# An fp32 hybrid encoder layer: four raw weight slots, operands one a unit, later low parts

## The chip, the cores and the metric

The kernel runs on one core of a Trainium2 chip. The metric is the device time of one execution in microseconds (us); lower is better. Five engines run side by side and meet at semaphores: TensorE (PE) multiplies, VectorE (DVE), ScalarE (ACT) and GpSimd (POOL) work on elements, SyncE (SP) issues transfers.

## The reference

One layer over 2048 prompt frames with 16 meta tokens ahead of them and 32 frames of a running stream, 1024 channels, fp32:

```python
proj = rmsnorm(x) @ w_in                      # x_a, x_b, g_a, g_b, 1024 columns each
y_a  = rg_lru(conv4(x_a))                     # two 128-wide gates a head, then a scan over time
y_b  = pool_mix(x_b)                          # window means 2, 4, 8, 16, then a grouped product
x    = x + (sig(g_A) * (y_a @ w_br_a) + sig(g_B) * (y_b @ w_br_b)) @ w_out
g, u = split(rmsnorm(x) @ w_gu)               # 2816 columns each
x    = x + (silu(g) * u) @ w_down
y    = rmsnorm(x) * final_g
```

Outputs are y and the convolution, scan and pooling states of both streams.

## The kernel before

**Split products.** Every operand is cut into a high part (rounded to fp32r) and a low part (the rest), and a product takes three matmuls a 128-deep step: high by high, high by low, low by high. Weights arrive raw from memory by SP into `wraw`, three slots of 1024 columns; ACT makes the high part (L878, `split_hi`), DVE the low part (L1720, `split_lo`) in `wring`, three places of 1024 columns (a fourth, `wextra`, in the mixer), or in `wlast`, four places of 768 columns over the same memory. PE waits for the low part. SP sends for raw slot n when the low part of slot n-3 is made. ACT may write a place of the ring when PE has used it up; these waits stand in the program at `ahead` and `ahead_of`, right where the product that frees the place ends.

**Mixer.** Five blocks of 416 or 432 columns, each with the stages xa (convolution input), gates, ga, gb, a, xb, b and o, eight products of 24 matmuls each. In stage o (output projection) of a block but the last, ACT per product m waits for DVE's addition of the product to `main` (L1857), squares the sum for the next norm (`square`, L909), makes the next block's high operand (`normed`, L931), and splits a weight. DVE per product splits a weight, makes the next operand and the low part of the one before (`normalize`, L1360, L1364), adds (L1857), and adds up the square (`square_sum`, L1342).

**Feed-forward.** Three tiles of two halves of 348 or 346 columns; the products of 2 by 2 blocks take 7 block products, not 8 (`PROD`). `gate_up(s, p)` is one of 11 pairs of hidden tiles: 7 products (units) of 24 matmuls, k = 0 to 6. ACT and DVE drain them (`tap_out` L1106, `add_out` L1625), take the SiLU (L1147) and make the seven hidden operands with high and low parts in `hcomb` (DVE L1672 to L1698; the fourth and fifth low parts are L1696 and L1698). `down(s, g)` follows pair 2g+2 and uses pairs 2g and 2g+1, in 14 units of 12 matmuls; the last, g = 4, uses three pairs with the 768-wide weights, 14 units of 18. It starts before pair 10 is ready: for its first three units PE makes the sums over two pairs, then it waits for pair 10's parts and adds the third. `add_down` (L1711) adds each unit to `xacc`. PSUM is four pairs of banks in turn, so a unit needs the addition of the unit four before it.

**Beside it.** While pair 10 and the last down group run, the next tile's seven operands `ycomb` are made from `ys` in memory: POOL loads quarters of `ys` into `work` (L609), DVE makes four differences (`operand_diff`: T1 L1578, T3 L1580, T2 L1583, T4 L1586), ACT the high parts (`operand_hi`, L1095), DVE the low parts (`operand_lo`, L1569). The tables `BESIDE_B`, `BESIDE_O`, `BESIDE_GU` and `BESIDE_DN` say at which unit. The last quarter is sent for when the sixth low part is made. In the first two pairs of a tile the norm of the tile before is finished: squares, a column sum on PE, a root, one reciprocal of 692 columns (`norm_invert`, L1612), and eight scalings (`finish`, L1617) at the units in `FINISH`.

The lines in `down(s, 4)` that set how much PE does ahead of the wait for pair 10:

```python
                    for k, mp in steps[:3]:
                        hold(("dn", s, g, mp, k, 0))
                        part(k, mp, (0, 1))
                pe.wait_ge(h_hi, 4 * n)
                pe.wait_ge(h_lo, 4 * n)
```

## Time and profile before

| what | value |
| --- | --- |
| time, median of 3 runs | 2750.82 us (2748.52 to 2753.92) |
| the profiled execution: time, span | 2748.8 us, 2747.0 us |
| PE matmuls | 15404, busy 2681.8 us (98% of the span) |
| DVE, ACT, POOL busy | 2059.0 (75%), 1358.9 (49%), 192.9 us (7%) |
| granted TensorE clock, mean | 0.995 |
| transfers | 486.10 MB, mean 177 GB/s |
| chain that ended last | PE 76%, DVE 12%, issue 5%, ACT 4%, DMA 2% |

The span runs from the first to the last instruction. A row of the timeline gives start, duration, engine, line, operation, tiles written and read, and in square brackets the idle time of that engine ahead of it with what ended it. "issue" is time that the profile puts down to no one.

### The profile page before, as it was taken

What the parts mean: (1) busy time and instruction counts of PE and PEld (TensorE: products, weight loads), DVE (VectorE), ACT (ScalarE), POOL (GpSimd) and SP (SyncE); (2) the same over time, 40 slices, a digit from 0 to 9 for tenths busy, and PEclk for the clock granted to TensorE, in tenths of its full rate; (3) what the DMA queues carried; (4) which work ended last, traced back from release to release, by engine and by line L of the source; (5) the groups of instructions that cost most, each with busy time, mean ns of one, the idle gap of its engine ahead of it and who ended that gap; (6) DMA issues with size and microseconds to landing.
All of it is one profiled execution on the core that took longest, in us unless ns stands there. A gap on an engine that the chain in (4) does not pass through costs nothing.

```text
span 2747.0 us, 39191 instructions
## 1 busy us (share of the span) xinstructions
PE 2681.8 (98%) x15404; PEld 2651.8 (97%) x15404; DVE 2059.0 (75%) x2723; ACT 1358.9 (49%) x1822; POOL 192.9 (7%) x369
## 2 busy tenths in 40 slices
PE   8999999999999999999999999999999999999995
PEld 7999999999999999999999999999999999999995
DVE  7868787788878877887777676688667688676666
ACT  6743484358436743663454344454434345344442
POOL 2000101020101011101100000001000000000000
PEclk9999999999999999999999999999999999999998
DMA  7453567546765767566564444456444454644443
GB/s 241 132 186 115 192 222 268 190 162 228 253 202 172 235 220 233 172 231 210 199 205 133 144 138 138 141 160 235 130 144 136 139 160 163 207 137 139 131 131 99
DMA packets 149254, 486.10 MB, mean 177 GB/s; under 512 B 16464, under 2 KB 34000, under 8 KB 149072
## 3 DMA queue, kind: packets, MB, share of 16 engines
q1 hardware_dynamic: 106224, 345.21, 38.5%
q0 software_dynamic: 32336, 121.92, 12.9%
q10 hardware_dynamic: 10512, 16.46, 2.0%
q8 instruction: 124, 2.03, 0.3%
q14 instruction: 58, 0.48, 0.1%
HBM read 419.01 MB, written 64.51 MB: 176 GB/s over the span
## 4 chain that ended last, share of the span: by engine, by line
PE 76%; DVE 12%; issue 5%; ACT 4%; DMA 2%; SPq 0%; DVEq 0%; ACTq 0%
PE ps L704 75%; DVE wring L1720 2%; ACT wring L878 1%; DVE work L1672 1%; DMA work<-ys 1%; ACT work L1147 1%; DVE work L1625 1%; DVE ga L1841 1%; DVE xacc L1711 1%; DVE work L1674 1%; DVE tmp L1839 1%; DMA wraw<-dwm 1%; DMA wraw<-draw 1%; DVE hcomb L1678 1%; DVE nrstd L1612 0%
## 5 line engine op out<-in xcount | busy, mean ns | idle before, releaser
L704 PE MATMUL ps<-ycomb,wring 128*128 128x346 f32 (+1 forms) x5544 | 884.7, 321 | 9.6 <-DVE wring L1720 5.7
L704 PEld LDWEIGHTS ps<-ycomb,wring 128*128 128x128 f32 x5544 | 880.8, 188 | 11.6 <-DVE wring L1720 6.9
L1720 DVE TENSOR_TENSOR wring<-wraw,wring 128x1024 fp32r<-128x1024 f32 x529 | 644.9, 1220 | 261.8 <-ACT wring L878 260.1
L878 ACT ACTIVATE wring<-wraw 128x1024 fp32r<-128x1024 f32 x529 | 557.1, 1054 | 443.9 <-PE ps L704 422.6
L704 PE MATMUL ps<-xhi,wring 128*128 128x416 f32 (+1 forms) x1728 | 478.3, 353 | 11.8 <-DVE wring L1720 8.9
L704 PE MATMUL ps<-yhi,wring 128*128 128x416 f32 x1568 | 429.5, 351 | 0.4 <-DVE ylo L1364 0.4
L704 PEld LDWEIGHTS ps<-xhi,wring 128*128 128x128 f32 x1728 | 326.4, 189 | 16.6 <-issue 12.4
L704 PE MATMUL ps<-hcomb,wring 128*128 128x346 f32 (+1 forms) x2016 | 325.6, 322 | 4.7 <-DVE xacc L1711 4.7
L704 PEld LDWEIGHTS ps<-hcomb,wring 128*128 128x128 f32 x2016 | 320.6, 188 | 8.0 <-DVE xacc L1711 8.0
L704 PE MATMUL ps<-xlo,wring 128*128 128x416 f32 (+1 forms) x864 | 305.2, 353 | 0.0
L704 PEld LDWEIGHTS ps<-yhi,wring 128*128 128x128 f32 x1568 | 294.3, 188 | 2.8 <-issue 0.7
L704 PE MATMUL ps<-ylo,wring 128*128 128x416 f32 x784 | 275.1, 351 | 0.0
L1711 DVE TENSOR_TENSOR xacc<-ps,xacc 128x692 f32<-128x692 f32 (+1 forms) x210 | 179.0, 872 | 39.0 <-PE ps L704 39.0
L1106 ACT ACTIVATE work<-ps 128x692 f32<-128x692 f32 (+1 forms) x99 | 74.1, 748 | 193.9 <-PE ps L704 193.7
L704 PEld LDWEIGHTS ps<-xlo,wring 128*128 128x128 f32 x864 | 163.1, 189 | 2.8
L704 PE MATMUL ps<-xhi,wextra 128*128 128x416 f32 (+1 forms) x576 | 162.1, 352 | 0.0
L704 PEld LDWEIGHTS ps<-ylo,wring 128*128 128x128 f32 x784 | 147.1, 188 | 1.7
L1625 DVE TENSOR_TENSOR work<-ps,work 128x692 f32<-128x692 f32 (+1 forms) x99 | 86.8, 877 | 71.0 <-PE ps L704 71.0
L704 PE MATMUL ps<-yhi,wextra 128*128 128x416 f32 x480 | 134.7, 352 | 0.0
L704 PE MATMUL ps<-hcomb,wlast 128*128 128x346 f32 (+1 forms) x756 | 122.7, 322 | 7.8 <-DVE wlast L1720 5.0
L704 PEld LDWEIGHTS ps<-hcomb,wlast 128*128 128x128 f32 x756 | 119.9, 188 | 10.4 <-issue 10.4
L704 PEld LDWEIGHTS ps<-xhi,wextra 128*128 128x128 f32 x576 | 108.2, 188 | 1.4
(236 smaller groups left out, 2922.8 us busy)
## 6 DMA issues: line engine op xcount, KB each, us to landing
wraw<-dwm SPq DMA_DIRECT2D x247, 512.0 KB, 3.9
wraw<-sgu SPq DMA_DIRECT2D x132, 512.0 KB, 3.3
wraw<-graw SPq DMA_DIRECT2D x99, 512.0 KB, 3.5
wraw<-sdn SPq DMA_DIRECT2D x48, 512.0 KB, 3.6
pbuf<-graw POOLq DMA_DIRECT2D x22, 1024.0 KB, 7.5
sgu<-pbuf POOLq DMA_DIRECT2D x22, 1024.0 KB, 6.1
wraw<-fused SPq DMA_DIRECT2D x40, 512.0 KB, 3.3
wraw<-draw SPq DMA_DIRECT2D x36, 512.0 KB, 3.7
```

Of the source, the lines that this page charges most:

```text
L704: mm = nc.tensor.matmul(out, wt[:, c * P:(c + 1) * P], x, start=(first and q == 0), stop=(last and q == 2), skip_group_check=chain)
L878: A(ring(n)[:, 0, 0:c], wraw[:, n % RAW, 0:c], ACT.Copy, scale=cst[:, PSC, name[2]:name[2] + 1] if name[0] == "w" else 1.0).then_inc(w_hi, 1)
L1106: A(work[:, first:first + 8:7, 0:TH[s]], both(name, TH[s]), ACT.Copy).then_inc(cleared[BANK[name] // 2], 1)
L1147: A(work[:, 0:3, 0:w], work[:, 0:3, 0:w], ACT.Silu).then_inc(silu3, 1)
L1625: V.tensor_tensor(c, both(name, TH[s]), c, ADD).then_inc(cleared[BANK[name] // 2], 1)
L1672: V.tensor_tensor(work[:, 7:10, 0:w], work[:, 7:10, 0:w], work[:, 0:3, 0:w], MUL).then_inc(h_mult, 1)
L1674: V.tensor_tensor(work[:, 3:5, 0:w], work[:, 8:10, 0:w], work[:, 7:9, 0:w], SUB).then_inc(h_diff, 1)
L1678: V.tensor_tensor(hl[:, 0:2, :], work[:, 7:10:2, 0:w], hh[:, 0:2, :].bitcast(f32), SUB).then_inc(h_lo, 1)
L1711: V.tensor_tensor(out, both(name, w), out, ADD).then_inc(cleared[BANK[name] // 2], 1)
L1720: V.tensor_tensor(ring(n)[:, 1, 0:c], wraw[:, n % RAW, 0:c], ring(n)[:, 0, 0:c].bitcast(f32), SUB).then_inc(w_lo, 1)
L1839: V.tensor_tensor(tmp[:, 3 + 4 * (m % 2), 0:LW], bank(name)[:, 0:LW], gb[:, m, 0:LW], MUL).then_inc(drained[BANK[name]], 1)
L1841: V.tensor_tensor(ga[:, m, :], ga[:, m, :], tmp[:, 3 + 4 * (m % 2), 0:LW], ADD).then_inc(merged, 1)
```

## The change

1. `wraw` gets a second view, `rawlast`, of four slots of 768 columns in the same 12 units of memory. A planner (`places`) gives each slot its place and the slot whose low part must be made before it is loaded. For the last down group that is four slots back, not three; with four raw semaphores by n % 4.
2. In `down(s, 4)` PE takes four units with two pairs ahead of the wait for pair 10, not three.
3. `hidden_rest` holds the last two low parts of a pair. Where a down group of two pairs follows the pair, DVE runs it behind that group's first two additions.
4. The operand tables: operand 0 a unit earlier, one entry a unit in the last down group and in stage o, and T4 moved to the next tile's first unit, operand 6 to its third. In pairs' units DVE takes operands behind `add_out`; in the last down group and the last block's stage o ACT takes them behind the weight split.
5. In stage o of blocks 0 to 3 ACT squares behind the next operand and the split, and DVE adds the square up one product later.
6. The reciprocal is taken in two halves of 346 or 348, at units (1, 0) and (1, 1) of a tile, and in a row at the end of the program; `FINISH` starts one unit later for its first four entries. The last block's last quarter is sent for behind store 6, not 5.

The core of the diff; its two parts on `ahead` are ACT's, in stage o and in the last down group:

```diff
-FINISH = {(1, 1): (0,), (1, 2): (1,), (1, 3): (2,), (1, 4): (3,), (2, 0): (4, 5), (2, 1): (6, 7)}
+FINISH = {(1, 2): (0,), (1, 3): (1,), (1, 4): (2,), (1, 5): (3,), (2, 0): (4, 5), (2, 1): (6, 7)}
-BESIDE_O = {2: ("T1", "T3"), 3: ("T2", 4), 4: (2,), 5: (3,), 7: ("T4",)}
-BESIDE_GU = {2: (0,), 4: (5,)}
-BESIDE_DN = {1: (1,), 4: ("T1", "T3"), 5: ("T2", 4), 7: (2,), 8: (3,), 11: ("T4",)}
+BESIDE_O = {2: ("T1", "T3"), 3: ("T2",), 4: (4,), 5: (2,), 6: (3,)}
+BESIDE_GU = {1: (0,), 4: (5,)}
+BESIDE_DN = {1: (1,), 3: ("T1",), 4: ("T3",), 5: ("T2",), 6: (4,), 7: (2,), 8: (3,)}
...
-PLACE, PREV = ring_places()
+PLACE, PREV = places(16, RING, True)
 RELEASE = list(itertools.accumulate(PREV, max))
+RAW_PLACE, RAW_PREV = places(12, RAW, False)
+RAW_RELEASE = list(itertools.accumulate(RAW_PREV, max))
...
-                if n >= RAW:
-                    sp.wait_ge(w_lo, n - RAW + 1)
+                if RAW_RELEASE[n] >= 0:
+                    sp.wait_ge(w_lo, RAW_RELEASE[n] + 1)
...
-                    for k, mp in steps[:3]:
+                    for k, mp in steps[:4]:
...
-                    if width == 3 and i < 3:
+                    if width == 3 and i < 4:
...
+                    if b < NB - 1 and m < KT - 1:
+                        normed(b + 1, m + 1)
+                    ahead(b, "o", m)
                     if b < NB - 1:
                         act.wait_ge(*drain(("o", b, m)))
                         square("n2", b, m, main[:, m, :])
-                        if m < KT - 1:
-                            normed(b + 1, m + 1)
                     else:
                         operands(0, BESIDE_O, m)
-                    ahead(b, "o", m)
...
+                        ahead_of("dn", s, i, j)
                         if s < NT - 1 and i == LASTG:
                             operands(s + 1, BESIDE_DN, j)
-                        ahead_of("dn", s, i, j)
...
-            def norm_invert(s):
-                w = 2 * TH[s]
+            def norm_invert(s, half):
+                w = TH[s]
                 dve.wait_ge(*clear(("n3", s, 0)))
-                V.reciprocal(nrstd[:, 0:w], nrstd[:, 0:w]).then_inc(n_rstd, 1)
+                V.reciprocal(nrstd[:, half * w:half * w + w], nrstd[:, half * w:half * w + w]).then_inc(n_rstd, 1)
...
                 if (p, k) == (0, 0):
+                    operand_diff(s, "T4")
+                elif (p, k) == (0, 2):
                     operand_lo(s, 6)
...
+                if early or not before_dn(s, p):
+                    hidden_rest(s, p)
...
                             add_down(s, i, j, 0)
                             add_down(s, i, j, 1)
+                            if j == 0:
+                                hidden_rest(s, 2 * i + 2)
```

Three places of DVE's order, in tile 0. First, the end of pair 10 (`ycomb` operand low parts, `work<-ps` the additions of `add_out`, `wlast` the last down group's weights), before:

```order
L1569 TENSOR_TENSOR ycomb<-work,ycomb 128x4x346
L1720 TENSOR_TENSOR wring<-wraw,wring 128x1024 x2
L1569 TENSOR_TENSOR ycomb<-work,ycomb 128x4x346
L1625 TENSOR_TENSOR work<-ps,work 128x2x348 x2
L1672 TENSOR_TENSOR work<-work 128x1044
```

and now:

```order
L1580 TENSOR_TENSOR ycomb<-work,ycomb 128x4x346
L1743 TENSOR_TENSOR wring<-wraw,wring 128x1024 x3
L1636 TENSOR_TENSOR work<-ps,work 128x2x348
L1580 TENSOR_TENSOR ycomb<-work,ycomb 128x4x346
L1636 TENSOR_TENSOR work<-ps,work 128x2x348
L1685 TENSOR_TENSOR work<-work 128x1044
```

The second operand low part stood ahead of both additions and stands between them. Second, pair 2's end and the first down group, before:

```order
L1720 TENSOR_TENSOR wring<-wraw,wring 128x1024
L1696 TENSOR_TENSOR hcomb<-work,hcomb 128x348
L1698 TENSOR_TENSOR hcomb<-work,hcomb 128x348
L1711 TENSOR_TENSOR xacc<-ps,xacc 128x2x348 x2
L1720 TENSOR_TENSOR wring<-wraw,wring 128x1024
```

and now:

```order
L1743 TENSOR_TENSOR wring<-wraw,wring 128x1024
L1734 TENSOR_TENSOR xacc<-ps,xacc 128x2x348 x2
L1719 TENSOR_TENSOR hcomb<-work,hcomb 128x348
L1721 TENSOR_TENSOR hcomb<-work,hcomb 128x348
L1743 TENSOR_TENSOR wring<-wraw,wring 128x1024
```

The two low parts went behind the two additions. Third, the end of the last down group and the start of tile 1 (`work<-work 128x4x346` is T4), before:

```order
L1711 TENSOR_TENSOR xacc<-ps,xacc 128x2x348 x2
L1586 TENSOR_TENSOR work<-work 128x4x346
L1720 TENSOR_TENSOR wring<-wraw,wring 128x1024
L1711 TENSOR_TENSOR xacc<-ps,xacc 128x2x348
L1720 TENSOR_TENSOR wring<-wraw,wring 128x1024
L1711 TENSOR_TENSOR xacc<-ps,xacc 128x2x348
```

and now:

```order
L1734 TENSOR_TENSOR xacc<-ps,xacc 128x2x348 x2
L1743 TENSOR_TENSOR wring<-wraw,wring 128x1024
L1734 TENSOR_TENSOR xacc<-ps,xacc 128x2x348
L1743 TENSOR_TENSOR wring<-wraw,wring 128x1024
L1734 TENSOR_TENSOR xacc<-ps,xacc 128x2x348
L1743 TENSOR_TENSOR wring<-wraw,wring 128x1024
L1597 TENSOR_TENSOR work<-work 128x4x346
```

T4 went behind all the group's additions and three splits of the next tile's weights.

## Rows read from the trace of the kernel before

**Rows 1.** Who PE waited for, whole span: us in total, times, longest us.
```profile
PE ps L704 <- DVE wring L1720: 14.6, 5, 8.9
PE ps L742 <- issue: 11.0, 1, 11.0
PE ps L704 <- DVE xacc L1711: 4.7, 12, 1.3
PE ps L704 <- DVE xlo L1364: 3.0, 2, 2.5
PE ps L704 <- DVE ylo L1364: 0.4, 1, 0.4
```

**Rows 2.** Chain that ended last: a stretch of ten mixer products.
```profile
462.50 45.36 PE ps L704 x240
```

**Rows 3.** DVE's timeline, stage o of block 3.
```profile
1097.31 0.58 DVE L1857 TENSOR_TENSOR main<-ps,main 128x416 f32<-128x416 f32 x1
...
1102.21 0.58 DVE L1857 TENSOR_TENSOR main<-ps,main 128x416 f32<-128x416 f32 x1
...
1104.89 1.23 DVE L1720 TENSOR_TENSOR wring<-wraw,wring 128x1024 fp32r<-128x1024 f32 x1 [0.89 <-ACT wring L878]
```

**Rows 4.** ACT's timeline, the same product.
```profile
1102.82 0.55 ACT L909 ACTIVATE sq<-main 128x416 f32<-128x416 f32 x1 [2.85 <-DVE main L1857]
...
1103.81 1.04 ACT L878 ACTIVATE wring<-wraw 128x1024 fp32r<-128x1024 f32 x1
```

**Rows 5.** DVE's timeline, end of pair 2 in tile 0.
```profile
1455.08 0.51 DVE L1696 TENSOR_TENSOR hcomb<-work,hcomb 128x348 fp32r<-128x348 f32 x1
...
1455.94 1.67 DVE L1711 TENSOR_TENSOR xacc<-ps,xacc 128x696 f32<-128x696 f32 x2
```

**Rows 6.** PE's timeline, first down group of tile 0.
```profile
1456.87 19.42 PE L704 MATMUL ps<-hcomb,wring 128*128 128x348 f32 x120 [0.32 <-DVE xacc L1711]
```

**Rows 7.** PE's timeline, pair 10 of tile 0 to tile 1's first pair.
```profile
1769.86 4.07 PE L704 MATMUL ps<-ycomb,wring 128*128 128x348 f32 x24 [1.35 <-DVE work L1625]
1775.45 5.99 PE L704 MATMUL ps<-hcomb,wlast 128*128 128x348 f32 x36 [1.52 <-DVE wlast L1720]
1782.74 20.28 PE L704 MATMUL ps<-hcomb,wlast 128*128 128x348 f32 x126 [1.30 <-issue]
1804.02 14.61 PE L704 MATMUL ps<-hcomb,wlast 128*128 128x348 f32 x90 [1.01 <-DVE wlast L1720]
1820.52 23.11 PE L704 MATMUL ps<-ycomb,wring 128*128 128x346 f32 x144 [1.88 <-DVE wring L1720]
```

**Rows 8.** DVE's timeline, the same stretch.
```profile
1767.32 1.60 DVE L1569 TENSOR_TENSOR ycomb<-work,ycomb 128x1384 fp32r<-128x1384 f32 x1 [3.46 <-ACT ycomb L1095]
1768.84 1.67 DVE L1625 TENSOR_TENSOR work<-ps,work 128x696 f32<-128x696 f32 x2
...
1807.76 0.95 DVE L1720 TENSOR_TENSOR wlast<-wraw,wlast 128x768 fp32r<-128x768 f32 x1
...
1810.92 0.95 DVE L1720 TENSOR_TENSOR wlast<-wraw,wlast 128x768 fp32r<-128x768 f32 x1
...
1817.73 1.60 DVE L1586 TENSOR_TENSOR work<-work 128x1384 f32<-128x1384 f32 x1 [2.62 <-DMA work<-ys]
```

**Rows 9.** ACT's timeline, the same stretch.
```profile
1778.68 0.84 ACT L878 ACTIVATE wlast<-wraw 128x768 fp32r<-128x768 f32 x1 [3.82 <-DMA wraw<-draw]
...
1800.01 1.36 ACT L1095 ACTIVATE ycomb<-work 128x1384 fp32r<-128x1384 f32 x1 [6.85 <-DVE work L1583]
```

**Rows 10.** POOL's timeline, the last quarter of `ys` for tile 1.
```profile
1811.30 0.75 POOL L609 DMA_DIRECT2D work<-ys  x1 [26.87 <-DVE ycomb L1569]
```

**Rows 11.** Groups by line and shape, PE in tiles 1 and 2: busy, mean ns, idle before.
```profile
L704 PE MATMUL ps<-ycomb,wring 128*128 128x346 f32 x3696 | 589.1, 321 | 7.3 <-DVE wring L1720 5.7 <-DVE work L1625 1.6
...
L704 PE MATMUL ps<-hcomb,wlast 128*128 128x346 f32 x504 | 81.8, 322 | 4.0 <-DVE wlast L1720 2.5 <-issue 1.4
```

**Rows 12.** DVE's timeline, the reciprocal in tile 1.
```profile
1854.94 4.50 DVE L1612 RECIPROCAL nrstd<-nrstd 128x696 f32<-128x696 f32 x1 [0.42 <-ACT nrstd L1122]
```

More of the change, by code:

```diff
@@ L205, in slot_width, with places @@
     return 768 if name[0] == "dn" and dn_units(name[2]) == 14 else KT * P
-LANDED = [16 * (n // RAW + 1) for n in range(NS)]
+LANDED = [16 * (n // 4 + 1) for n in range(NS)]
 NARROW = SLOT[("b", NB - 1, 0)]
-def ring_places():
-    last, places, before = [-1] * 16, [], []
+def places(units, wide, spare):
+    last, where, before = [-1] * units, [], []
     for n in range(NS):
         each = 3 if slot_width(n) == 768 else 4
-        spans = [range(each * q, each * q + each) for q in range(4 if each == 3 or n < NARROW else 3)]
+        spans = [range(each * q, each * q + each) for q in range(4 if each == 3 else wide + (spare and n < NARROW))]
         held = [max(last[u] for u in span) for span in spans]
         q = held.index(min(held))
-        places.append(q)
+        where.append(q)
         before.append(held[q])
@@ L224, in ring_places @@
             last[u] = n
-    return places, before
-PLACE, PREV = ring_places()
+    return where, before
+PLACE, PREV = places(16, RING, True)
 RELEASE = list(itertools.accumulate(PREV, max))
+RAW_PLACE, RAW_PREV = places(12, RAW, False)
+RAW_RELEASE = list(itertools.accumulate(RAW_PREV, max))
 def splits_after(k):
@@ L877, in split_hi @@
                 name, c = SLOTS[n], slot_width(n)
-                A(ring(n)[:, 0, 0:c], wraw[:, n % RAW, 0:c], ACT.Copy,
+                A(ring(n)[:, 0, 0:c], raw_of(n)[:, 0:c], ACT.Copy,
                   scale=cst[:, PSC, name[2]:name[2] + 1] if name[0] == "w" else 1.0).then_inc(w_hi, 1)
@@ L1661, in gate_up @@
                     beside(s, p, k)
-                    if p == PAIRS - 1 and s < NT - 1:
-                        operands(s + 1, BESIDE_GU, k)
                     if k == 1:
@@ L1676, in gate_up @@
                         V.tensor_tensor(work[:, 5, 0:w], work[:, 9, 0:w], work[:, 3, 0:w], SUB).then_inc(h_diff, 1)
+                    if p == PAIRS - 1 and s < NT - 1:
+                        operands(s + 1, BESIDE_GU, k)
                 dve.wait_ge(h_hi, 4 * n + 1)
@@ L1879, in _ @@
             norm_rest(NT - 1)
-            norm_invert(NT - 1)
+            for half in range(2):
+                norm_invert(NT - 1, half)
             for i in range(KT):
```

47 lines of the change are left out of this document (30 added, 17 removed).

## The prediction

> **What bounds the kernel now.** I read first how busy each engine is: PE computes during 98% of the span, and the change takes no matmul away and adds none. So all it can give is a part of PE's idle time, and the view of who PE waited for is the one to read. Of its long entries two lie outside the change: 8.9 us for the first weights of the program, and the 11.0 us before the last column sum, in which squares are added up on DVE [rows 1]. What is left are short waits, and each has its place in a timeline. There the reader looks at three things: which instruction ended PE's wait, what stood ahead of it on its own in-order engine, and what that one waited for. PE's pace between waits is needed as well: 240 matmuls of the mixer take 45.36 us, so a product of 24 takes 4.54 us [rows 2]; in the feed-forward 24 take about 3.86 us and 126 take 20.28 us, 0.161 us each, so a unit of 18 takes 2.90 us [rows 7].
>
> **Stage o of blocks 0 to 3.** DVE's additions to main follow each other at 4.90 us (1097.31 to 1102.21) [rows 3], PE's products at 4.54 us [rows 2]. The cause is a ring of waits over two engines: DVE adds, ACT squares the sum and only then makes the next operand and splits the weight (1102.82, split at 1103.81) [rows 4], DVE waits for that split (1104.89) [rows 3], then makes a low part and adds the next product. Each product falls back 0.36 us, eight make 2.9 us, and PE pays where the next block needs the last low part: 3.0 us in two waits and 0.4 us in a third [rows 1]. With the change ACT's split stands ahead of the square, so it starts when PE frees the place, about 0.6 us of addition and 0.5 us of square earlier, and the addition is no longer in the ring. From PE's end of a product, DVE is through with split, operand, low part and addition after about 1.0 + 1.2 + 1.1 + 0.6 = 3.9 us, under 4.54. I take all **3.4 us**; the bounds are 0 and 3.4. The added-up square is a product later, and its column sum is due only in the next block's gates, two stages on, which hides it.
>
> **Down groups of two pairs.** Twelve waits, 4.7 us in all, one of 1.3 and eleven of 0.24 to 0.38 [rows 1, 6]. PE's fifth unit needs the first addition; it starts at 1455.94 because the two low parts stand before it from 1455.08, 0.86 us [rows 5]. Moved behind, they free the bank 0.86 us sooner, and the small waits end. DVE's next split comes at the same time as before, since the same work precedes it. Who needs the two low parts? PE in the next down group, some 27 us on, and ACT's next use of that buffer a pair on. The long wait (1.3) keeps at least 0.4. I take **4.2 us**; bounds 3.3 and 4.7.
>
> **Tile 0, pair 10 and last down group.** Four waits: 1.35, 1.52, 1.30 and 1.01 us, 5.18 together [rows 7].
> - 1.35: unit 6 needs the addition of unit 4, which started at 1768.84, behind an operand's low part (1767.32) that had waited 3.46 us through ACT for its quarter [rows 8]. PE stopped at 1768.5 (1769.86 less 1.35), so unit 4 had ended a unit earlier, near 1764.7. Now the addition stands first, and the quarter is sent for a unit (3.86 us) sooner. This wait goes.
> - 1.52: this is the chain from unit 5's addition over SiLU, product and differences to the weight split. It is the second of the two at 1768.84 [rows 8] and so began near 1769.6, while unit 5 had ended at 1768.5. Freed of the first, it and the chain start 1.1 us sooner, and unit 6 ends 1.35 us sooner. PE starts the group at 1774.35, not 1775.45, after a wait of 1.95 us: the wait of 1.35 is gone, the one behind it grows, and 1.1 us is won.
> - 1.30: PE had three units of 12 ahead (5.99 us) and then waited for pair 10's last low part. That part was late because DVE's fourth weight split stood before it, and ACT's half of that split had waited 3.82 us for the raw weights [rows 9], which SP may send for only once the first wlast low part is made. With the fourth slot they are sent for one low part earlier and lie there in time. PE got the last part at 1782.74; with the chain 1.1 us sooner it is there by 1781.6 even if nothing of the transfer's wait is saved, and four units of 12 (twice 3.86 us) keep PE until 1774.35 + 7.7 = 1782.1. This wait goes.
> - 1.01: two differences in a row and operand 4 right behind the third; ACT stood 6.85 us for T2 with a weight split queued behind it [rows 9]. Now the split stands first and there is one operand a unit. What is late next is DVE: a split, an addition and an operand follow each other at 3.16 us (1807.76 to 1810.92) [rows 8] against PE's 2.90, from unit 3 to unit 8. Counting from the group's start, the split for unit 12 is ready near 35.1 us and PE wants it at 34.8. I put 0.4 us here; bounds 0 and 1.5.
>
> So 5.18 becomes 2.35: **2.8 us**.
>
> **Tiles 1 and 2, the same place.** Waits of 1.6 (addition), 2.5 (wlast) and 1.4 us (pair 10's parts), 5.5 together [rows 11]. In tile 1 the first weights of the group are split early, so both additions one operand sooner let the whole chain start over 2 us sooner; what stays is about 0.45 for the third unit's weights and 0.4 of DVE's lag. Tile 2 has no operands and keeps one 0.5, and loses the wait for pair 10. 5.5 becomes 1.35: **4.1 us**; bounds 2.5 and 4.8.
>
> **First pairs of tiles 1 and 2.** Four waits for weights, 5.7 us [rows 11]. Two (the longest 1.88 [rows 7]) stand behind T4, for which DVE waited 2.62 us on the quarter sent for at 1811.30 and landed at 1817.7 [rows 8, 10]. T4 now stands behind three splits. PE needs it, through ACT's tap_out, before unit 2 of the tile, 7.7 us in; that leaves over 5 us. Two stand behind the reciprocal of 4.50 us [rows 12]; a split between two halves of 2.25 us comes that much sooner, and the second half still ends before the next split is due. I take all **5.7 us**; bounds 3.5 and 5.7. FINISH a unit later puts a scaling ahead of an addition in unit 5, whose result is due only units later. In tile 0 the last quarter leaves over 4 us later than before, because operand 3 went from product 5 of stage o to 6 and behind ACT's split. From the end of product 6: split 1.0 [rows 4], operand high 1.4 [rows 9] and low 1.6, quarter 6.4 [rows 8, 10], T4 1.6 and tap_out some 0.8 (half of the two additions of 1.67) make 12.8 us. PE wants it after product 7, units 0 and 1 and whatever it waits at the tile's start: 4.5 + 7.7 = 12.2 us and that wait, which is DVE's last addition of stage o, some 0.7 us. That just fits: 0, at most 1 us lost.
>
> **The program's end.** Two halves of the reciprocal for one. Two instructions of 348 columns start 0.43 us apart [rows 5], one of 696 takes 0.83: the second instruction costs 0.03 us by these starts, 0.2 by whole durations (twice 0.51 less 0.83), and I take **0.1 us lost**. The Trainium skill (VectorE: DVE Perf Modes, on the TRN2 errata) speaks against such cuts: an instruction from SBUF pays a fixed cost each time, some 150 cycles, which at the engine's 0.96 GHz would be 0.16 us lost; the rows stand nearer to the lower value, and the sum would move by less than 0.1.
>
> **The sum.** 3.4 + 4.2 + 2.8 + 4.1 + 5.7 - 0.1 = 20.1 us. Against the profiled execution's own 2748.8 us that gives 2728.7. The median of the runs shown stands 2.0 us above it, and the same gain from there gives 2730.7. I forecast **2729.6 us**, between the two. A measurement of this kernel can tell about 0.2% (5.5 us) from no change.
>
> **Rivals.**
> - *DVE becomes the bound in the last groups.* DVE is busy for most of that stretch, and one operand a unit at 3.16 against 2.90 us leaves no air. If raw weights and semaphores add 0.3 us a unit over six units, some 2 us of waits in each of tiles 0 and 1 come back, with 1 to 2 us more where the first pairs are as full. For it: the lag is real. Against it: four ring places, three units of slack. 2729.6 + 6 = about 2735.5. Chance 0.22.
> - *The change doesn't do what it says.* The stage-o ring stays at 4.90 us since ACT's in-order queue still holds the square ahead of the next operand (3.4 us not won), and the two reciprocal halves leave the split late (2 us), and the down groups wait for the next addition (2 us). About 2737. Chance 0.07.
> - *Slower: T4 blocks DVE at the start of each tile.* T4 now sits in the pair in which DVE has the norm's sums too, and DVE is in order: while it waits for the quarter, splits and additions wait. Sums, splits and additions behind it have about 1 us of slack by unit 4. The quarter took 6.4 us alone [rows 10]. If it took 15 us because four raw loads and it were under way together, each of three tiles would lose 5 to 9 us: 20 gained, up to 27 lost, about 2756. It decides from a landing of some 13 us on. The Trainium skill (DMA: Bandwidth & Descriptors, on issuing engines) says that transfers from SP, ACT and POOL run on the same 16 engines and interleave, so a deeper raw queue could lengthen the quarter; 6.4 us here, with raw loads beside it, speaks against more than a few us. Chance 0.03.
> - Forecast, within 5 us: 0.66; the rest (0.02) is a small gain of under 5 us from several misses.
>
> **Range.** The low end takes all upper bounds (about 2 us more won) from the profiled execution: 2726. The high end takes the lower bounds and the first two rivals: 2739. Faster 0.94, same 0.03, slower 0.03.
>
> **What the changed profile would show.** DVE's additions in stage o 4.5 us apart and no wait for L1375's low part; no waits of 0.3 us for L1734 in down groups; 48 matmuls, not 36, at the head of the last group with no "issue" wait behind them, and a wait near 2 us ahead of it in tile 0 only; no wait at a tile's start; DVE's idle before T4 small in tiles 1 and 2 and some 3 us in tile 0; PE busy unchanged near 2682. I am wrong if new waits of over 1 us stand in units 8 to 13 of the last group, or in units 3 to 6 of a tile's first pair.

## The result, and the profile after

The changed kernel takes **2726.18 us** (median of 5 runs, 2723.72 to 2727.25); the kernel before, run beside it, 2749.32 us (5 runs, 2748.52 to 2753.92). The ratio is 0.991, with a 95% interval of 0.9897 to 0.9924. A second set of five runs gave 2726.32 us and 0.9917 (0.9903 to 0.993). So the change is faster by some 23 us. I had forecast 2729.6 with a low end of 2726: the direction was right, and the waits ended for the reasons given, but the price that the sum puts on a wait was too low. The central value is 3.4 us too high, and the measured time lies at the very low end of the range.

The profiled execution took 2727.25 us, with a span of 2725.5; that is 21.5 us less than the profiled execution of before (span 2747.0). The page's first part:

```profile
PE 2678.8 (98%) x15404; PEld 2652.8 (97%) x15404; DVE 2056.2 (75%) x2726; ACT 1360.2 (50%) x1822; POOL 191.2 (7%) x369
```

PE's busy time was 2681.8 us before. So of the 21.5 us, 18.5 left PE's idle time (2747.0 - 2681.8 = 65.2 before, 2725.5 - 2678.8 = 46.7 now) and 3.0 left its *busy* time, although the matmuls are the same 15,404. That second number is what the forecast has no term for: it had PE's busy time unchanged near 2682.

Who PE waited for, whole span (us in total, times, longest; answers to [rows 1]):

```profile
PE ps L753 <- issue: 11.0, 1, 11.0
PE ps L715 <- DVE wring L1743: 9.6, 2, 8.9
PE ps L715 <- DVE wlast L1743: 3.1, 3, 2.1
PE ps L715 <- ACT tmp L1031: 2.6, 1, 2.6
PE ps L715 <- DVE main L1880: 1.4, 1, 1.4
...
PE ps L715 <- DVE xacc L1734: 0.6, 1, 0.6
```

The waits for an operand's low part in stage o are gone, those for the down group's first addition went from 4.7 us in twelve to 0.6 in one, those for split weights (wring) from 14.6 in five to 9.6 in two, of which 8.9 is the program's first weights. The line with main is new in size (0.89 us before): the start of tile 0.

DVE's timeline in stage o of block 3 (answers to [rows 3]): the additions are 4.54 us apart, PE's own pace.

```profile
1095.23 0.59 DVE L1880 TENSOR_TENSOR main<-ps,main 128x416 f32<-128x416 f32 x1 [1.09 <-PE ps L715]
...
1099.77 0.59 DVE L1880 TENSOR_TENSOR main<-ps,main 128x416 f32<-128x416 f32 x1 [1.59 <-PE ps L715]
```

What released DVE is now PE, not ACT's split. DVE at the end of pair 2 (answers to [rows 5]); the addition stands ahead of the two low parts, and PE runs through:

```profile
1453.72 1.66 DVE L1734 TENSOR_TENSOR xacc<-ps,xacc 128x696 f32<-128x696 f32 x2
1455.30 0.51 DVE L1719 TENSOR_TENSOR hcomb<-work,hcomb 128x348 fp32r<-128x348 f32 x1
```

PE's timeline from tile 0's start to the last group of tile 2 (answers to [rows 7]; start, length, count, and in brackets the idle time before):

```profile
1365.11 23.15 PE L715 MATMUL ps<-ycomb,wring 128*128 128x348 f32 x144 [1.44 <-DVE main L1880]
1389.12 15.51 PE L715 MATMUL ps<-ycomb,wring 128*128 128x348 f32 x96 [0.21 <-DVE work L1636]
1405.28 6.95 PE L715 MATMUL ps<-ycomb,wring 128*128 128x348 f32 x42 [0.65 <-DVE wring L1743]
...
1770.74 41.30 PE L715 MATMUL ps<-hcomb,wlast 128*128 128x348 f32 x252 [2.05 <-DVE wlast L1743]
1811.87 23.00 PE L715 MATMUL ps<-ycomb,wring 128*128 128x346 f32 x144
...
2218.31 37.38 PE L715 MATMUL ps<-hcomb,wlast 128*128 128x346 f32 x228 [0.50 <-DVE wlast L1743]
...
2661.09 36.39 PE L715 MATMUL ps<-hcomb,wlast 128*128 128x346 f32 x228 [0.50 <-DVE wlast L1743]
```

There is one wait of 2.05 us ahead of tile 0's last group, then all 252 matmuls stand in one row, and tile 1 begins without a wait. The three last rows hold something smaller: the same 228 matmuls take 37.38 us in tile 1, where DVE makes the next tile's operands beside them, and 36.39 in tile 2, where it makes none. In tile 1, PE starts a matmul 0.39 us behind the one before, and the next 0.24 us behind that, at 2229.11, 2246.59 and 2249.75 us. The usual distance is 0.16, so each of the three places costs 0.31 us. Each stands just behind the end of a weight split on DVE, and DVE needs 3.17 us a unit there:

```profile
2245.49 0.95 DVE L1743 TENSOR_TENSOR wlast<-rawlast,wlast 128x768 fp32r<-128x768 f32 x1
...
2248.66 0.95 DVE L1743 TENSOR_TENSOR wlast<-rawlast,wlast 128x768 fp32r<-128x768 f32 x1
```

So PE does wait for DVE there, in gaps of 0.08 us that the timeline draws as no idle time. And DVE's timeline at tile 1's reciprocal (answers to [rows 12]):

```profile
1847.13 2.33 DVE L1623 RECIPROCAL nrstd<-nrstd 128x348 f32<-128x348 f32 x1 [0.21 <-ACT nrstd L1133]
1849.38 1.16 DVE L1743 TENSOR_TENSOR wring<-wraw,wring 128x1024 fp32r<-128x1024 f32 x1
1850.46 2.31 DVE L1623 RECIPROCAL nrstd<-nrstd 128x348 f32<-128x348 f32 x1
```

To see where the 21.5 us come from, I paired each matmul of one trace with the same matmul of the other and took the difference of their starts; where that difference steps, time was won or lost. Against the terms of the forecast:

| place | forecast, us | steps of the starts, us |
|---|---|---|
| stage o of blocks 0 to 3 | 3.4 | 0.66 + 0.68 + 2.80 = 4.1 |
| down groups of two pairs | 4.2 | ten of 0.51 to 0.60, one of 1.21, one of -0.19: 6.7 |
| tile 0, pair 10 and last group | 2.8 | 3.0 |
| tiles 1 and 2, the same place | 4.1 | 3.3 + 0.9 = 4.2 |
| first pairs of tiles 1 and 2 | 5.7 | 3.1 + 3.3 = 6.4 |
| tile 0's start and first pair | 0 | -0.53 - 0.69 - 0.90 = -2.1 |
| elsewhere | -0.1 | -0.7 (-0.8 of it in the first 100 us) |
| sum | 20.1 | 21.6 |

The terms of the last groups are net: what DVE's lag gives back there is taken off. The first 100 us are no term of the change. They hold 1.8 us less in a second profile of the same kernel (the next experiment).

### The profile page after: what moved, and what is told of

Its sections match the earlier page's. It is cut to its first block, busy times and chain, and to the rows that moved or that the text cites. A ratio compares the mean times of both kernels' runs of the same rounds, so it can differ in the third digit from the quotient of the medians.

```text
span 2725.5 us, 39194 instructions
## 1 busy us (share of the span) xinstructions
PE 2678.8 (98%) x15404; PEld 2652.8 (97%) x15404; DVE 2056.2 (75%) x2726; ACT 1360.2 (50%) x1822; POOL 191.2 (7%) x369
## 4 chain that ended last, share of the span: by engine, by line
PE 91%; DVE 4%; DMA 2%; issue 1%; ACT 1%; SPq 0%; DVEq 0%; ACTq 0%
PE ps L715 91%; DVE wring L1743 1%; DMA wraw<-draw 1%; DVE xacc L1628 0%; ACT wring L889 0%; DMA wraw<-graw 0%; DVE work L1685 0%; DVE work L1636 0%; ACT work L1158 0%; DVE work L1687 0%; DVE ntot L1613 0%; DVE hcomb L1693 0%; DMA wraw<-dwm 0%; DMA work<-ys 0%; DVE hcomb L1706 0%
```

## The experiments

There are two theories of why more was won than the idle rows hold. **Theory H**: ending a wait gives back its idle row *and* a fixed quarter of a microsecond around it. The rival: the idle rows are the whole price, and the rest is chance, or belongs to some other edit. Two more questions came from the table: whether tile 0's first pair really loses 2 us, and which edits carry which term.

**The same kernel again** (no edit).

> The changed kernel once more, unedited, timed against the kernel before. Theory A (the gain is the profiled 21.5 us, and the 23.1 us of the medians is how runs fall): gain between 20.5 and 24 us again, the profile's waits at the same places, PE's waits in the first pair of tile 0 (0.21 and 0.65 us idle) there again. Theory B (those waits are a chance of this one execution's transfers): they are gone, and the span is about 1.5 us shorter.

Measured: 2726.32 us (5 runs, 2725.36 to 2728.14), span 2723.6. PE's waits show no entry inside tile 0's first pair, so the waits of 0.21 and 0.65 us there do not belong to every execution; the 1.44 at the tile's start is there again:

```profile
1363.43 8.82 PE L715 MATMUL ps<-ycomb,wring 128*128 128x348 f32 x54 [1.44 <-DVE main L1880]
...
1767.53 42.84 PE L715 MATMUL ps<-hcomb,wlast 128*128 128x348 f32 x252 [2.05 <-DVE wlast L1743]
```

The second row is a surprise. The wait is the same 2.05 us, but the 252 matmuls behind it take 42.84 us, not 41.30. More on this below. The one wait left for a down group's addition moved as well, with no edit: it stands at 1901 us in the first profile (0.59 us) and at 2342 us in this one (0.68 us).

**Hidden low parts back in line.** Every pair's last two low parts stand before the down group's first additions again.

```diff
-                if early or not before_dn(s, p):
-                    hidden_rest(s, p)
+                hidden_rest(s, p)
...
-                            if j == 0:
-                                hidden_rest(s, 2 * i + 2)
```

> The changed kernel with the two last low parts of a pair back ahead of the down group's additions (all 12 groups of two pairs). Theory H (a wait of PE costs its idle row plus about 0.25 us, since the profile lets the last matmul end late and the first ones after a wait run slower): the groups lose 12 x 0.56, 6 to 7 us in all, while the idle rows show about 4. Theory R (a wait costs what its idle row says): 3.5 to 4.2 us lost.

Measured: 2734.76 us (one run), span 2733.0. The waits are back as they were:

```profile
PE ps L715 <- DVE xacc L1733: 5.0, 12, 1.4
```

That is 4.4 us of idle time more than in the changed kernel (5.0 less 0.6). The starts of the matmuls step by 0.51 to 0.62 at ten of the twelve places, by 1.27 at one and by nothing at one (where the changed kernel has its own wait of 0.6), 7.0 us in all. So this edit is worth 7.0 us and not 4.4, as Theory H has it (4.4 and eleven times 0.25 are 7.15). The total is 8.6 us above the changed kernel's median. The 1.6 that the 7.0 leave are about what the slower stretch at 1771 us, told of below, takes by the starts (1.5).

How a wait costs more than its row can be read in the kernel *before*, at the place of [rows 6], when PE's timeline is cut into narrow windows:

```profile
1456.24 0.32 PE L704 MATMUL ps<-hcomb,wring 128*128 128x348 f32 x1
1456.87 0.43 PE L704 MATMUL ps<-hcomb,wring 128*128 128x348 f32 x1 [0.32 <-DVE xacc L1711]
1457.14 0.80 PE L704 MATMUL ps<-hcomb,wring 128*128 128x348 f32 x4
```

Undisturbed matmuls start 0.16 us apart and each is drawn 0.32 long, two overlapping. Around the wait the starts are 0.63 and 0.27 apart: 0.90 us for two steps that should take 0.32, a loss of 0.58. The idle row says 0.32. The other 0.26 is the half of the last matmul that nothing overlaps (0.16) and the slower first one behind (0.11), and both are booked as busy. The same reckoning, from 570 us to the last column sum of that trace, gives the same for all 29 waits that have no second one within a few matmuls: their idle rows are 0.24 to 2.55 us, and each costs 0.21 to 0.29 us more than its row. It is a fixed amount and does not grow with the wait. So a part of the price of a wait stands in PE's busy time. That time fell by only 3.0 us with the change, since the new waits and DVE's lag, most of which is booked as busy, put some back.

**The square ahead of the operand again, in stage o.**

```diff
                 for m in range(KT):
-                    if b < NB - 1 and m < KT - 1:
-                        normed(b + 1, m + 1)
-                    ahead(b, "o", m)
...
                         square("n2", b, m, main[:, m, :])
+                        if m < KT - 1:
+                            normed(b + 1, m + 1)
+                        ahead(b, "o", m)
```

(and DVE adds up the square of the same product, not of the one before).

> The changed kernel with stage o's order of before (square ahead of the next operand and the split; square added up at once). Theory H: three waits of 0.4, 0.4 and 2.5 us idle come back and PE loses 4.1 us. Theory R: 3.4 us. Both: DVE's additions to main 4.9 us apart.

Measured: 2734.37 us (one run), span 2732.6. The ring is back: DVE's additions stand at 1098.77 and 1103.66, 4.89 us apart, and the waits are those of before.

```profile
PE ps L715 <- DVE xlo L1377: 3.0, 2, 2.6
...
PE ps L715 <- DVE ylo L1377: 0.4, 1, 0.4
```

The starts step by 0.62, 0.68 and 2.83 us, 4.1 in all, where the rows hold 3.4: again a quarter of a microsecond each. Behind the 2.58 us wait PE ran slowly for some microseconds (PEclk in the window, the granted clock in parts of full speed):

```profile
1106.00:1112.00 6.00, 3.72 (x12) 3.59 (x13) 4.67 (x6) 3.65 (x6) 2.16 (x5) 0.72 0.39 134
```

That adds about 1.6 us, and a like stretch behind the wait at 1776 us about 1.5. A third, near 85 us, lasted longer than in the changed kernel's first profile (1.6 us). So the total of 8.2 over the changed kernel is twice the term.

**One reciprocal again.**

```diff
-                w = TH[s]
+                w = 2 * TH[s]
...
-                elif s and (p, k) == (1, 1):
-                    norm_invert(s - 1, 1)
```

> The changed kernel with the norm's reciprocal in one instruction again, FINISH left as changed. Theory H: two waits of 1.1 us idle come back in the first pairs of tiles 1 and 2 and cost 2 x 1.3 = 2.6 us; the end of the program is 0.05 to 0.2 us shorter. Theory R: 2.1 us lost. A rival (the scalings a unit later did it): no wait comes back, time as the changed kernel.

Measured: 2732.55 us (one run), span 2730.8. Two waits for wring come back, 2.14 us in tile 1 and 1.5 in tile 2:

```profile
1854.06 6.15 PE L715 MATMUL ps<-ycomb,wring 128*128 128x346 f32 x37 [2.14 <-DVE wring L1741]
```

By the starts they cost 2.4 and 1.8 us, 4.2 in all. Both theories had put the rows at 1.1 us each, so both sums were too low; beyond the rows each wait cost 0.25 us again. By whole durations two halves (2.33 and 2.31 us) take 0.14 longer than the 4.50 of one. By starts they do not: the split stands 2.25 us behind the first half, and the two in a row at the program's end take what the one takes there in the kernel of this run.

```profile
2710.92 4.49 DVE L1623 RECIPROCAL nrstd<-nrstd 128x346 f32<-128x346 f32 x2 [2.50 <-ACT nrstd L1133]
```

```profile
2716.26 4.48 DVE L1623 RECIPROCAL nrstd<-nrstd 128x692 f32<-128x692 f32 x1 [2.50 <-ACT nrstd L1133]
```

The first row is the changed kernel's, the second this run's. So the cut buys 4.2 us for 0.01. The total of 6.4 us over the changed kernel holds a slower stretch behind the 2.06 us wait as well, 1.5 us.

**T4 of tiles 1 and 2 back to the last down group.**

```diff
-BESIDE_DN = {1: (1,), 3: ("T1",), 4: ("T3",), 5: ("T2",), 6: (4,), 7: (2,), 8: (3,)}
+BESIDE_DN = {1: (1,), 3: ("T1",), 4: ("T3",), 5: ("T2",), 6: (4,), 7: (2,), 8: (3,), 11: ("T4",)}
...
-                if (p, k) == (0, 0):
+                if (p, k) == (0, 0) and not s:
                     operand_diff(s, "T4")
```

> Only the difference T4 of tiles 1 and 2 goes back behind unit 11 of the last down group, ahead of the tile's first splits. Before, two of four waits at the start of each tile stood behind it; putting the reciprocal back alone cost 2.40 and 1.70 us by the starts of the matmuls. Theory H (idle rows and 0.25 us a wait; what the whole place gained was 3.31 and 3.11 us): the rest comes back, 0.9 and 1.4 us, and at most the whole of the two longer waits, 1.9 + 0.25 and 1.3 + 0.25: 2.3 to 3.7 us, about 2728.5 to 2729.9 us. Rival (with the other changes DVE is early enough to wait for the quarter at no cost): within 1 us of 2726.2.

Measured: 2729.57 us (one run), span 2727.8. In tile 1's last group DVE stands before T4, and the split that PE needs first is behind it:

```profile
2253.13 1.60 DVE L1597 TENSOR_TENSOR work<-work 128x1384 f32<-128x1384 f32 x1 [3.29 <-DMA work<-ys]
2254.64 1.22 DVE L1743 TENSOR_TENSOR wring<-wraw,wring 128x1024 fp32r<-128x1024 f32 x1
```

```profile
2255.92 14.40 PE L715 MATMUL ps<-ycomb,wring 128*128 128x346 f32 x81 [3.23 <-DVE wring L1743]
```

The waits cost about 1.1 us at tile 1 and 3.5 at tile 2, and the slower stretch behind the second some 1.3 more. The 4.6 us lie above the 2.3 to 3.7 expected. That the total of 2729.57 falls into the range expected for it is luck: this execution has no slower stretch at 85 or 1770 us, as most have. PE's second wait is longer than any here before the change (the rows of before show 1.71 at that place), since the sooner the rest runs, the longer DVE stands before a quarter whose time is set by its own chain. The two edits on the first pairs therefore do not add up to 6.4; each alone leaves the other's wait to be paid in full.

**Three raw slots again.**

```diff
-                if RAW_RELEASE[n] >= 0:
-                    sp.wait_ge(w_lo, RAW_RELEASE[n] + 1)
+                if n >= RAW:
+                    sp.wait_ge(w_lo, n - RAW + 1)
...
-            return rawlast[:, RAW_PLACE[n]] if slot_width(n) == 768 else wraw[:, RAW_PLACE[n]]
+            return wraw[:, n % RAW, 0:768] if slot_width(n) == 768 else wraw[:, n % RAW]
```

> The raw weights go back to three slots of 1,024; the four units of 12 at the head of the last group and all else stay as changed. My prediction said that the fourth slot only spares ACT its wait for raw weights and that tile 0's wait of 1.30 us for pair 10's last part would end without it, through the fourth unit and the sooner chain. Theory A (as predicted, the slot is cover that is not needed): within 1.5 us of 2726.2. Theory B (with three slots ACT waits some 3 us for the raw weights at each last group and each first pair, and DVE's splits and parts behind it are late): waits of 0.5 to 1.5 us come back at the head of the last group in tiles 0 and 1 and in the first pairs, 2729 to 2732 us.

Measured: 2724.77 us (one run), span 2723.0, and behind the program's start PE's waits are those of the changed kernel's second profile to 0.1 us. The total lies 1.4 us below the changed kernel's median; the first 100 us, where this profile has no slower stretch, account for that and more. The fourth slot, the longest part of the diff, brings nothing that shows. The prediction had counted on it only as cover that was not needed.

**Three units of 12 ahead, not four.**

```diff
-                    for k, mp in steps[:4]:
+                    for k, mp in steps[:3]:
```

> Three units of 12 ahead of pair 10's last low part again, with four raw slots. Theory A (the fourth unit is what covers the part): waits come back behind the third unit, about 1.0 us in tile 0 and 1.2 to 1.4 in tiles 1 and 2 less whatever the sooner chain saves, 0.25 us more each: 2.0 to 4.5 us in all, 2728.2 to 2730.7 us. Theory B (the chain is so much sooner that three units cover it): no wait, within 1 us of 2726.2.

Measured: 2724.48 us (one run), span 2722.7. The waits are there and the time isn't longer. The total is not the edit's worth, though: this is one of only two profiles here in which PE runs through from its first product to the last without a slower stretch (told of below). So the place itself has to be read:

```profile
1767.59 6.00 PE L715 MATMUL ps<-hcomb,wlast 128*128 128x348 f32 x36 [2.05 <-DVE wlast L1743]
1773.94 34.69 PE L715 MATMUL ps<-hcomb,wlast 128*128 128x348 f32 x216 [0.35 <-issue]
1808.47 23.00 PE L715 MATMUL ps<-ycomb,wring 128*128 128x346 f32 x144
...
2216.92 34.45 PE L715 MATMUL ps<-hcomb,wlast 128*128 128x346 f32 x216 [0.68 <-issue]
...
2660.29 34.45 PE L715 MATMUL ps<-hcomb,wlast 128*128 128x346 f32 x216 [0.68 <-issue]
```

Tile 0's group runs from 1767.59 to 1808.47, 40.88 us; in the changed kernel it took 1811.87 - 1770.74 = 41.13. Here the 216 matmuls take 34.45 us in tile 1 and in tile 2 alike, while with four units ahead tile 1 needed 0.99 us more than tile 2 for the same 228. So in tiles 0 and 1 the fourth unit saves PE a wait, PE then runs up to DVE, and DVE's operands make it lose as much again in pieces too small for an idle row. Only in tile 2, without operands, does it keep 0.9 us. By the starts, going back to three units wins 0.25 us in tile 0 and 0.1 in tile 1 and costs 0.9 in tile 2: 0.5 us in all. Both theories fell: the wait comes back, and ending it is worth little.

**The old units for the next tile's operands.**

```diff
-BESIDE_GU = {1: (0,), 4: (5,)}
-BESIDE_DN = {1: (1,), 3: ("T1",), 4: ("T3",), 5: ("T2",), 6: (4,), 7: (2,), 8: (3,)}
+BESIDE_GU = {2: (0,), 4: (5,)}
+BESIDE_DN = {1: (1,), 4: ("T1", "T3"), 5: ("T2", 4), 7: (2,), 8: (3,)}
```

> Only the units beside which the operands of the next tile are made go back (two differences in a row and an operand right behind the third in the down group, operand 0 in unit 2 of pair 10); four raw slots, hidden low parts and the split reciprocal stay. My prediction put the end of the waits of 1.35 us (unit 6 of pair 10, shared with 1.52) and of 1.01 us (third difference) in tile 0 down to this part. If so both come back in tile 0 and the one of pair 10 in tile 1: 1.35 and 1.0 us in tile 0 and about 0.8 in tile 1, with 0.25 each, some 3.9 us above the changed kernel, 2730. Rival (the raw slots or the hidden low parts ended them, not the units): no wait for wring L1743's differences comes back, within 1 us of 2726.2.

Measured: 2734.13 us (one run), span 2732.3: 8 us over the changed kernel where I expected 4.

```profile
PE ps L715 <- DVE wlast L1743: 9.7, 6, 2.6
```

The wait for the third difference was 1.01 us before the change [rows 7]; here it is 2.61 in tile 0 and 2.61 in tile 1. DVE made T2 and then stood for operand 4, with the split that PE needed behind it:

```profile
1793.46 1.60 DVE L1594 TENSOR_TENSOR work<-work 128x1384 f32<-128x1384 f32 x1
1796.55 1.60 DVE L1580 TENSOR_TENSOR ycomb<-work,ycomb 128x1384 fp32r<-128x1384 f32 x1 [1.49 <-ACT ycomb L1106]
1798.07 0.95 DVE L1743 TENSOR_TENSOR wlast<-rawlast,wlast 128x768 fp32r<-128x768 f32 x1
```

Nearly 3 of the 8 us are slower stretches behind both long waits (granted clock 0.57 in 1799 to 1803 us), 1.5 and 1.3 us by the starts. An edit's worth depends on the others: with the earlier waits gone this one alone would have eaten a third of the gain.

**Tile 0's table of before.** Operand 3 behind product 5 of stage o again, T4 behind product 7, the last quarter sent a product earlier.

```diff
-BESIDE_O = {2: ("T1", "T3"), 3: ("T2",), 4: (4,), 5: (2,), 6: (3,)}
+BESIDE_O = {2: ("T1", "T3"), 3: ("T2", 4), 4: (2,), 5: (3,), 7: ("T4",)}
```

> Only tile 0's way into the feed-forward goes back to the order before: operand 3 behind product 5 of stage o, T4 behind product 7, the last quarter sent for a product earlier; all else as changed. Theory A (the change loses about 0.6 us at the start of tile 0 and about 1.4 us more in its first pair, because operand 3 and T4 stand in DVE's way there): the matmuls of tile 0's first pair start 0.6 to 2.1 us sooner than in the changed kernel, total 2724.2 to 2725.7 us against 2726.2. Theory B (what differed inside the first pair was one execution's chance; a second profile of the changed kernel had no wait there): 0.5 to 0.7 us, the start of the tile alone, about 2725.6. If my prediction's 0 was right: 2726.2.

Measured: 2725.62 us (4 runs, 2724.87 to 2727.54), span 2723.6.

```profile
1364.82 23.15 PE L715 MATMUL ps<-ycomb,wring 128*128 128x348 f32 x144 [0.89 <-DVE main L1880]
```

The wait at the start is 0.89 us again and the starts step by 0.56: so much the new table costs for certain. The wait for wring some 40 us on (0.65 us in the changed kernel's first profile) is in seven of the ten profiles that have the new table, with 0.2 to 0.65 us, and in neither of the two that have the old one. It adds up to 0.9 us in most executions, which two profiles cannot settle.

**The first split of pair 10 ahead of the SiLU and the product**, to beat both kernels.

```diff
+                        early = splits_after(SLOT[("gu", s, p, 5)])[:1] if p == PAIRS - 1 else []
+                        for q in early:
+                            split_hi(q)
...
+                        if p == PAIRS - 1:
+                            for q in splits_after(SLOT[("gu", s, p, 5)])[:1]:
+                                split_lo(q)
```

> In pair 10 of each tile both ACT and DVE make the first weight split that unit 5 frees before the SiLU and product of the pair's last part, so PE need not wait for it at the head of the last down group. Theory H (an ended wait gives its idle row and some 0.25 us of slower starts around it): the waits of 2.05, 0.5 and 0.5 us end, 3.05 + 3 x 0.25 = 3.8 us, about 2722.4 us. Naive (idle rows alone): 3.0 us, 2723.2. Theory C (the granted clock that fell to about half for some 3 us behind this wait, in one of two profiles of the changed kernel, falls because PE stood still there): with no wait of 2 us ahead no such stretch stands between 1765 and 1780 us, and the runs lie a further 0 to 1.6 us lower. Rival (the split put ahead only delays the SiLU and product, so pair 10's last low part is late): a wait of 1 to 2 us for it behind the first units of the group, total within 1 us of 2726.2.

Measured: **2722.00 us** (4 runs, 2719.51 to 2723.95), ratio to before 0.9893 (0.9877 to 0.991), span 2720.1. The wait of 2.05 us ahead of tile 0's group is gone. One of 0.50 is left two units on, and tiles 1 and 2 have none:

```profile
1764.65 4.37 PE L715 MATMUL ps<-hcomb,wlast 128*128 128x348 f32 x24
1769.52 20.72 PE L715 MATMUL ps<-hcomb,wlast 128*128 128x348 f32 x127 [0.50 <-DVE wlast L1755]
```

DVE's split now stands at 1761.97, between the addition and the SiLU's result, for which DVE stood idle there, and DVE waits 0.20 for that result instead of 1.21:

```profile
1761.04 0.88 DVE L1642 TENSOR_TENSOR work<-ps,work 128x696 f32<-128x696 f32 x1 [1.42 <-PE ps L715]
1761.97 0.96 DVE L1755 TENSOR_TENSOR wlast<-rawlast,wlast 128x768 fp32r<-128x768 f32 x1
1763.13 1.25 DVE L1697 TENSOR_TENSOR work<-work 128x1044 f32<-128x1044 f32 x1 [0.20 <-ACT work L1161]
```

The total is nearer to Theory H's 2722.4 than to the 2723.2 of idle rows alone, but it does not decide between them: the runs span 4.4 us, and the starts give less than either. The three places win 1.2, 0.8 and 0.9 us, 2.9 in all (a 0.50 us wait stayed in tile 0, which neither theory had), and in tile 1's first pair 0.7 us are lost again in pieces without an idle row (the run with one reciprocal has such pieces at the same place, so they may be chance). From pair 10 of tile 0 to the end this profile is 1.5 us shorter than the changed kernel's first, and 2.9 us shorter than its second, which has the slower stretch at 1768 us. The rest of the 4.2 us between the medians is not located; the profiles differ most in their first 100 us and in tile 0's first pair, where this edit does nothing.

**Both of these edits.**

> Both of the other two edits at once. If they are independent the gains add: 0.6 (start of tile 0) + 3.8 = 4.4 us, about 2721.8 us; up to 2720.0 if the first pair gives its 1.4 us too. If DVE is the common limit they give less than the sum: about 2723.

Measured: **2721.47 us** (4 runs, 2720.86 to 2724.11), ratio 0.9894 (0.9879 to 0.9909), span 2719.3. The median is 4.7 us below the changed kernel's. The intervals of the two ratios overlap (the changed kernel's starts at 0.9897), so by times alone the step over the changed kernel is likely, not proven; the traces show the waits gone (wlast 3.1 us in three, now 0.5 in one). Tile 0's table adds 0.5 us by the medians, less than such runs can tell. Tile 1's 252 matmuls take 41.37 us here and tile 2's 40.35: DVE's lag of 1.0 us is what is left in this group.

## Where the prediction was right, and the step that failed

**Right.** The view to read was who PE waits for, and each wait went for the reason given. Stage o runs at 4.54 us a product, released by PE. The additions ahead of the low parts ended the waits of 0.3 us. The wait ahead of tile 0's last group is 2.05 us (1.95 forecast), tiles 1 and 2 keep 0.50 (0.45), the 48 matmuls at the head have no wait behind them, no tile but the first begins with a wait, and DVE stands still for 3.6 us before T4 in tile 0 ("some 3") and not at all in tiles 1 and 2. The fourth raw slot was rightly booked at nothing. (The prediction calls the 6.4 us of the last quarter once "alone" and once "with raw loads beside it"; in the trace raw loads are under way beside it.)

**Wrong in size: every term that was read from idle rows.** The sum took the idle column as the price of a wait. A wait costs about 0.25 us more, and the change ended some 25 of them. Where waits are long that is a tenth; in the down groups, with waits of 0.3 us, it nearly doubles the term: 4.2 forecast with an upper bound of 4.7, 6.7 measured by the steps and 7.0 by undoing the edit. This is the step that failed: the price of a wait, taken as its idle row and no more. The upper bound of the term failed with it, and so did the sign "PE busy unchanged near 2682" (2678.8). Stage o (3.4, called the upper bound; 4.1) and the first pairs (5.7, also the upper bound; 6.4) failed in the same way. The two terms of the last groups came out near their forecasts (3.0 for 2.8, 4.2 for 4.1) only because DVE's lag, which was put too low, took back what the price had left out; that is luck. The five terms won exceed their forecasts by 4.2 us together (0.7 + 2.5 + 0.2 + 0.1 + 0.7), and the 2.1 us lost at tile 0's start hide half of that in the total. The range shows the same. Its upper bounds add up to 3.4 + 4.7 + 3.2 + 4.8 + 5.7 - 0.1 = 21.7 us, 1.6 more than the forecast and not "about 2", so by its own rule the low end was 2727.1 and not 2726, and the measured 2726.2 lies below it.

**Wrong the other way, and smaller.** Tile 0's way into the feed-forward was put at 0, at most 1 lost; it loses 0.5 to 0.6 us for certain, and more in most executions (2.1 us in the first profile), for another reason than the one I worked on. I followed the quarter; what costs for certain is that operand 3's low part and a split stand ahead of DVE's last addition of stage o, for which PE waits 1.44 us, not 0.89.

**DVE's lag in the last groups** was put at 0.4 us (bounds 0 and 1.5) and is 1.0: 37.38 less 36.39 in tile 1, and in tile 0 41.30 less 40.35, what 252 matmuls take without operands beside them (tile 2 of the kernel with both edits). The three places of 0.31 us in tile 1 are nearly all of it: waits with next to no idle row and the whole fixed price. It left no idle row of its own, so the rival that DVE becomes the bound was in part true: it is why the fourth unit ahead is worth nothing in two tiles of three. It did not bring waits of over 1 us in units 8 to 13, the sign that I had named.

**The reciprocal** was put at 0.1 us lost at the program's end. Two halves in a row take 4.49 us there and one whole 4.48, so the term is 0.01, near the 0.03 by starts. My estimate of 0.16 us from the Trainium skill (VectorE: DVE Perf Modes, on the TRN2 errata) is not borne out by these rows. It is a term of no weight.

**The level.** I set the forecast midway between the profiled execution and a median of three that lay 2 us above it. Nine further runs of the kernel before had a median of 2749.43, those run beside the later experiments 2749.77, and those beside the result 2749.32. The midpoint (2749.8) was thus right within 0.5 us, and the miss of 3.4 lies nearly all in the gain, 23.1 us for 20.1.

## What to carry to other kernels

Price a wait by the starts of the matmuls around it, not by its idle row: here the last one before and the first one behind it lose a quarter of a microsecond more, which matters where waits are many and short. Before you pay for an edit that ends a wait, look at who is next: the same matmuls beside and without the other engine's work (37.38 against 36.39 us) show a lag that no idle row shows, and that gives back what you win. And put work that waits for a transfer or another engine behind what the critical engine needs next; undoing one such order (the old units) cost 8 us in its one run, over 5 of them in longer waits, where the wait that it once stood for was 1.01 us.

## What the runs showed of the hardware

**The granted TensorE clock may fall behind a wait of 2 us.** The second profile of the changed kernel and the kernel with three units ahead reach tile 0's last group in the same way, with the same wait of 2.05 us. The windows from 1767 to 1772 us (columns: length, busy time and count of PE, PEld, DVE, ACT and POOL, then the granted clock in parts of full speed, DMA share, GB/s), of the one:

```profile
1767.00:1772.00 5.00, 4.47 (x18) 4.50 (x19) 4.97 (x8) 2.60 (x4) 0.00 (x0) 0.66 0.52 162
```

and of the other:

```profile
1767.00:1772.00 5.00, 4.41 (x28) 4.45 (x29) 4.96 (x8) 2.66 (x4) 0.00 (x0) 1.00 0.51 160
```

18 matmuls against 28 in 5 us: in the first, PE worked through a part of it at the lower level, 1.2 GHz, having just stood still for 2.05 us. The group took 42.84 us against 41.30 in the first profile, so it cost 1.5 us. Of the nine profiles that have this wait (2.05 or 2.06 us) ahead of the group five show the fall behind it, and four don't; of the two with the early split, where only 0.50 us is left, neither does. Behind the longer waits of the experiments (2.58, 2.61 twice, 3.23 us) the clock fell around the wait's end each time, but behind 2.33 us in the kernel with the old units and 2.14 in that with one reciprocal it did not, nor behind the 2.55 us of stage o in the kernel before. The Trainium skill (TensorE: Matmul & The Clock Gate, on the clock gate) says that the chip's looking at PE's activity runs freely and doesn't start with the kernel, so that the same kernel meets it differently from run to run; the rows above, the same wait with and without the fall, agree.

A wait that no experiment touches shows it too: every profile has one of 2.1 to 2.8 us for tmp that ends near 85 us. The clock is down to half for a stretch there in nine of the 13 profiles, those of the kernel before and of the changed kernel among them, and in four it is not (three raw slots, three units, the old T4, the early split). With the same length of wait, 2.77 us, in the kernel before:

```profile
85.00:90.00 5.00, 4.76 (x17) 4.57 (x18) 2.30 (x5) 5.00 (x10) 0.00 (x0) 0.66 0.01 3
```

and in that with the old T4:

```profile
85.00:90.00 5.00, 4.48 (x24) 4.36 (x25) 2.30 (x4) 5.00 (x10) 0.00 (x0) 1.00 0.00 0
```

So a wait's length alone does not decide it. At the end of the program, where PE stands still for 11.04 us, the clock is at half in all 13 (0.50 over 2702 to 2707 us in the changed kernel). That it is PE's standing still that brings the fall on fits every case here but was not tried by itself, and two profiles without the wait are few. It explains part of the spread between runs, and it makes one profile, or one run, of a kernel uncertain by some 1.5 us for each such wait. That is why the single runs above are judged by the starts and not by their totals.
